# A state space mixer that projects its time steps before the convolved tiles, and takes the output norm of four groups at once inside the next projection

## The chip, the cores and the metric

The kernel runs on one core of a Trainium2 chip. The metric is the device time of one execution in microseconds (us), the median of three runs. The engines are TensorE (PE, with PEld for its weight loads), VectorE (DVE), ScalarE (ACT), GpSimd (POOL) and SyncE (SP), which issues most of the DMAs.

## The reference, cut to what matters

Two transformer-like blocks are computed in one launch. The change lies in the mixer of the first block: 512 tokens (lat) and 256 context tokens (ctx), width 1024. All of it is in 32-bit floats.

```python
p_l = modulate(rmsnorm(h_lat, norm1[i]), sh1_l, sc1_l) @ w_in[i]
p_c = modulate(rmsnorm(h_ctx, norm1[i]), sh1_c, sc1_c) @ w_in[i]
# ssd_inputs, for both: gate z, convolved xbc, two sets of 16 step sizes
z = proj[..., :OFF_XBC]
xbc = jax.nn.silu(dwconv_centred(proj[..., OFF_XBC:OFF_DT], conv_w, conv_b))   # 5 taps
dt_f = jax.nn.softplus(dt_raw[..., :SSD_HEADS] + dt_bias[0])
dt_b = jax.nn.softplus(dt_raw[..., SSD_HEADS:] + dt_bias[1])
# ssd_scan in chunks of 128, forwards and backwards, from dt, a = dt * a_head, xs, B, C; then
o_ssd_l = group_rmsnorm((y + xs * d_skip) * jax.nn.silu(z), norm_g, SSD_GROUPS)  # 4 groups of 256
# hyena: another 3072 columns of the projection, 3-tap convolution, two long convolutions
o_hy_l = hyena(p_l[..., OFF_HY:], ...)
mix_l = jnp.concatenate([o_ssd_l, o_hy_l], axis=-1) @ w_out[i]
```

## The kernel before, in words

Activations lie with their features on the 128 partitions and the tokens along the row. A projection (`project`, L262 on) makes one tile of 128 output features: eight slices of 128 inputs, three matmuls in reduced fp32 for each (`trio`, L253 to L255), because the weights and the input are split into a high and a low part. The weight tile comes by DMA into `raw_ring` (six slots of 128x1024, filled by SP strictly in one order, `load_order`), ACT casts the high part (`Weights.hi`, L235), POOL subtracts for the low part (`Weights.lo`, L243), and the two stand in one of three `pair` buffers. `tile_order` gives each tile a lead: how many tiles ahead its split stands in the program. Each engine runs its own list in order and waits on counters of the others; `everyone(k, eng, stage)` makes an engine wait until all four have ended a stage.

The stages that matter here:

- **inproj** (functions `..._inproj`). PE projects eight tiles of the gate z, then sixteen tiles that are convolved (`win` 8 to 23), the first twelve for lat and ctx (512 + 256 columns), the last four for lat alone. For each of the sixteen, ACT copies the tile from PSUM to `raw` (L520), DVE runs the five taps (L431, L434), ACT applies Silu (L525 to L532), PE transposes the result (`turned`, L280), DVE copies it out (L418, L419, L422). ACT copies a tile only after the Silu of the tile before it. DVE also computes the modulation, 32 `step`s (L407), each reading one slot of the ring: eight between the end of the input's split and the convolved tiles, sixteen with the convolved tiles, eight (40 to 47) after them. Last comes `wdt`, the 32 columns of step sizes: projected by PE after `win` 23, bias on DVE (L448), transposed, and turned into softplus by a chain of DVE instructions of 192 columns (L452 to L478) with one Exp on ACT (L536). The next stage needs its result `a` at once.
- **ssd1, ssd2**: the scan. At its end `zT` holds the gated output (L703).
- **ssd**: the group norm of `zT`. ACT squares eight tiles (L785), PE multiplies them by a matrix of 1/256 so that every partition of a 128x512 bank holds the mean (L259, in full fp32), DVE adds epsilon (L797), ACT takes the root (L789), DVE takes four reciprocals (L802) and multiplies (L711). `scalar_norms`, `vector_norms` and `tensor_norms` are used again by the hyena part.
- **hyena**, first part: 24 more projected tiles, `win` 24 to 47, each copied by ACT (L1051) and convolved by DVE with three taps (L952, L954, L956). On two of them DVE also computes `angles` (L936 to L946). All four engines enter it through `everyone(..., "ssd")`. POOL first issues three DMAs for the transform matrices (`dft`, L1084). The weights of `win` 24 to 26 are split only behind that wait.

## Time and profile before

| | |
|---|---|
| median of 3 runs | 5046.19 us (5045.71 to 5047.88) |
| the profiled execution | 5075.65 us, of which its span is 5073.8 us |
| PE busy | 4531.9 us, 89% of the span |
| DVE busy | 2722.1 us, 54% |
| POOL busy | 1754.2 us, 35% |
| ACT busy | 1515.6 us, 30% |
| mean granted clock of PE, of 1 | 0.94 |

The stages of the mixer in that execution, in us from the start of the span: the gate's tiles to about 125, the convolved tiles to 278, the steps and what is left of inproj to 298, the scan to 459, the norm to 495, the 24 tiles of the hyena projection to 632. The times of single instructions below come from this one profiled execution, which is 0.6% longer than the median run.

### The profile page before, as it was taken

What the parts mean: (1) busy time and instruction counts of PE and PEld (TensorE: products, weight loads), DVE (VectorE), ACT (ScalarE), POOL (GpSimd) and SP (SyncE); (2) the same over time, 40 slices, a digit from 0 to 9 for tenths busy, and PEclk for the clock granted to TensorE, in tenths of its full rate; (3) what the DMA queues carried; (4) which work ended last, traced back from release to release, by engine and by line L of the source; (5) the groups of instructions that cost most, each with busy time, mean ns of one, the idle gap of its engine ahead of it and who ended that gap; (6) DMA issues with size and microseconds to landing.
All of it is one profiled execution on the core that took longest, in us unless ns stands there. A gap on an engine that the chain in (4) does not pass through costs nothing.

```text
span 5073.8 us, 51551 instructions
## 1 busy us (share of the span) xinstructions
PE 4531.9 (89%) x20654; PEld 3503.6 (69%) x20654; DVE 2722.1 (54%) x4692; ACT 1515.6 (30%) x2546; POOL 1754.2 (35%) x933
## 2 busy tenths in 40 slices
PE   7866988787669999999999979997999979986998
PEld 3755845356557888888888856666888857754886
DVE  3875745349887666654443334563443450485334
ACT  3211211034752222222222233443212122343222
POOL 2243432025964444444444421003223225102442
PEclk9987999898789999999999999988999989998999
DMA  5210200121235544444433210001122202101331
GB/s 203 96 67 31 92 29 17 62 72 46 117 155 197 171 161 166 164 155 166 171 136 121 100 37 16 13 1 50 55 63 63 63 29 63 34 1 54 92 96 49
DMA packets 170618, 440.76 MB, mean 87 GB/s; under 512 B 12203, under 2 KB 78955, under 8 KB 167436
## 3 DMA queue, kind: packets, MB, share of 16 engines
q1 hardware_dynamic: 168060, 422.61, 24.5%
q0 software_dynamic: 2320, 14.86, 0.8%
q8 instruction: 164, 2.69, 0.2%
q14 instruction: 74, 0.61, 0.0%
HBM read 401.77 MB, written 35.65 MB: 86 GB/s over the span
## 4 chain that ended last, share of the span: by engine, by line
PE 60%; DVE 7%; ACT 2%; issue 1%; DMA 0%; POOL 0%; DVEq 0%; ACTq 0%; POOLq 0%
PE psum L253 17%; PE psum L255 17%; PE psum L254 17%; PE psum L259 7%; DVE st L2112 2%; PE psum L280 1%; DVE Pd L2138 1%; DVE k L802 1%; DVE X L1785 0%; ACT P L2183 0%; DVE ffl L1725 0%; DVE Pe L2136 0%; DVE rstd L1765 0%; DVE X L1788 0%; DVE st L2119 0%
## 5 line engine op out<-in xcount | busy, mean ns | idle before, releaser
L243 POOL TENSOR_TENSOR pair<-raw_ring,pair 128x1024 fp32r<-128x1024 f32 (+1 forms) x503 | 1243.8, 2488 | 2297.2 <-ACT pair L235 2297.1
L235 ACT CAST pair<-raw_ring 128x1024 fp32r<-128x1024 f32 (+1 forms) x503 | 510.3, 1044 | 370.7 <-PE psum L255 321.7
L253 PE MATMUL psum<-pfh,pair 128*128 128x512 f32 x1152 | 460.0, 399 | 27.4 <-POOL pair L243 25.8
L1578 DVE SCALAR_TENSOR_TENSOR h<-psum,mods,h 128x512 f32<-128x512 f32 x512 | 373.0, 748 | 184.4 <-PE psum L255 182.9
L255 PE MATMUL psum<-pfh,pair 128*128 128x512 f32 x1152 | 458.8, 398 | 0.0
L254 PE MATMUL psum<-pfl,pair 128*128 128x512 f32 x1152 | 458.4, 398 | 0.0
L253 PE MATMUL psum<-ffh,pair 128*128 128x512 f32 (+1 forms) x1056 | 382.3, 362 | 45.3 <-DVE ffl L1725 45.3
L253 PE MATMUL psum<-Ah,pair 128*128 128x512 f32 x1024 | 408.6, 399 | 9.8 <-DVE h L1578 4.8
L255 PE MATMUL psum<-Ah,pair 128*128 128x512 f32 x1024 | 407.9, 398 | 0.0
L254 PE MATMUL psum<-Al,pair 128*128 128x512 f32 x1024 | 407.8, 398 | 0.0
L254 PE MATMUL psum<-ffl,pair 128*128 128x512 f32 (+1 forms) x1056 | 380.3, 360 | 0.0
L255 PE MATMUL psum<-ffh,pair 128*128 128x512 f32 (+1 forms) x1056 | 379.8, 360 | 0.0
L1636 ACT ACTIVATE gl<-psum 128x512 f32<-128x512 f32 x122 | 73.1, 599 | 832.6 <-PE psum L255 832.6
L1571 DVE TENSOR_TENSOR pr<-gl,Gb 128x512 f32<-128x512 f32 x128 | 91.4, 714 | 342.2 <-ACT gl L1636 324.3
L253 PEld LDWEIGHTS psum<-pfh,pair 128*128 128x128 f32 x1152 | 218.7, 190 | 79.3 <-issue 23.1
L259 PE MATMUL psum<-o,o 128*128 128x128 f32 x1024 | 177.1, 339 | 101.6 <-POOL o L1503 77.2
L253 PEld LDWEIGHTS psum<-ffh,pair 128*128 128x128 f32 x1056 | 200.6, 190 | 84.1 <-issue 39.1
L254 PEld LDWEIGHTS psum<-pfl,pair 128*128 128x128 f32 x1152 | 218.8, 190 | 50.5
L255 PEld LDWEIGHTS psum<-pfh,pair 128*128 128x128 f32 x1152 | 218.6, 190 | 50.5
L259 PEld LDWEIGHTS psum<-o,o 128*128 128x128 f32 x1024 | 161.4, 243 | 117.6 <-POOL o L1503 78.5
L1948 DVE SCALAR_TENSOR_TENSOR X<-psum,mods,X 128x512 f32<-128x512 f32 (+1 forms) x264 | 170.8, 661 | 121.0 <-PE psum L255 121.0
L253 PEld LDWEIGHTS psum<-Ah,pair 128*128 128x128 f32 x1024 | 194.4, 190 | 56.3 <-issue 9.6
(517 smaller groups left out, 9305.0 us busy)
## 6 DMA issues: line engine op xcount, KB each, us to landing
raw_ring<-wmod SPq DMA_DIRECT2D x144, 512.0 KB, 5.2
raw_ring<-peeru SPq DMA_DIRECT2D x128, 512.0 KB, 4.2
raw_ring<-peerv SPq DMA_DIRECT2D x128, 512.0 KB, 4.8
gates<-stage SPq DMA_DIRECT2D x16, 2048.0 KB, 6.4
Gb<-gates SPq DMA_DIRECT2D x32, 1024.0 KB, 9.2
raw_ring<-win SPq DMA_DIRECT2D x48, 512.0 KB, 4.4
raw_ring<-wgate SPq DMA_DIRECT2D x44, 512.0 KB, 3.5
raw_ring<-wup SPq DMA_DIRECT2D x44, 512.0 KB, 3.6
```

The source lines that it names most:

```text
L235: ac.e.copy(self.pair(t)[0], k.R.of(t)).then_inc(*k.A.up("hi", t))
L243: po.e.tensor_tensor(lo, k.R.of(t), hi.bitcast(F), ALU.subtract).then_inc(*k.G.up("lo", t))
L253: e.matmul(out, w[0], x[0], start=first, stop=False, skip_group_check=True)
L254: e.matmul(out, w[0], x[1], start=False, stop=False, skip_group_check=True)
L255: return e.matmul(out, w[1], x[0], start=False, stop=last, skip_group_check=True)
L259: return e.matmul(out, w, x, start=first, stop=last, skip_group_check=True)
L280: return e.transpose(out, src, k.sq["ident"][0:n, 0:n])
L1571: e.tensor_tensor(v3(y, 32), v3(x, 32), G4[:, :, n % 4, :], ALU.mult).then_inc(*V.up("act", n))
L1578: e.scalar_tensor_tensor(out=h[:, j, :], in0=B.of(("down", gi, j)), scalar=m[:, 40 + j, 0:1], in1=h[:, j, :], op0=ALU.mult, op1=ALU.add).t ...
L1636: e.activation(gelus(k, n), B.of((("U", n), 0)), AF.Gelu).then_inc(*A.up("gelu", n))
L1948: e.scalar_tensor_tensor(out=x, in0=B.of((key, "down", gi, q, s))[:, 0:b - a], scalar=m[:, 40 + q, s:s + 1], in1=x, op0=ALU.mult, op1=ALU. ...
L2112: e.tensor_reduce(s[:, 0:1], bank[:, 0:u.n], AX, ALU.max).then_inc(*V.up())
```

## The change

It does three things.

- `wdt` gets buffers of its own. It is loaded by SP behind `wmod` 47, ACT casts it after the eighth gate tile, POOL subtracts before the low part of the tile that `win` 8 asks for, and PE projects it ahead of `win` 8. Its transposes follow `win` 8. The short DVE part stands behind convolved tile 1, the long part behind tile 3, and ACT's Exp ahead of the copies of tile 3. The buffers of the chain move to `Btok`, which is written only from tile 8 on. Modulation steps 40 to 47 stand beside steps 16 to 23. With `wdt` out of `tile_order`, `win` 24 takes its place: it is split during inproj.
- The stage `ssd` is gone. The squares are taken by ACT after hyena tiles 0 and 1, in eight buffers of their own. `tensor_means` puts the means of the four groups on four partitions of one bank (behind tile 2), DVE adds epsilon (behind tile 3), ACT takes one root (behind tile 4), DVE one reciprocal of 4x512 (behind tile 5), `tensor_back` spreads each group's row over 128 partitions with four matmuls (behind tile 7), and DVE multiplies two tiles of `zT` behind each of tiles 8 to 11.
- PE enters hyena without a wait, the others wait for `ssd2`. The `dft` DMAs are issued by POOL behind tile 10, since the squares use that memory.

The core of the diff (the body of the step-size chain is the same in both, and only moved):

```diff
 def tensor_inproj(k, pe):
...
+    pe.wait_ge(k.G.at("lo", "wdt"))
+    for s, (a, b) in enumerate(SEG2):
+        bank = B.take(("wdt", s))
+        pe.wait_ge(B.free(("wdt", s)))
+        for q in range(8):
+            i = trio(e, bank[0:32, 0:b - a], [w[:, 32 * q:32 * q + 32] for w in k.wdt], k.fx(q, s), q == 0, q == 7)
+        i.then_inc(*P.up("wdt", s))
     for j in range(16):
         project(k, pe, ("win", 8 + j), k.fx, SEG2 if j < 12 else SEG1)
+        if j == 0:
+            bank = B.take("dtT")
+            pe.wait_ge(V.at("dtin", 1), B.free("dtT"))
...
-    project(k, pe, ("wdt",), k.fx, SEG2, M=32)
...
 def vector_inproj(k, dv):
...
     for j in range(8):
         step(16 + j)
+        step(40 + j)
...
+    dt_in()
     for j in range(16):
...
+        if j == 1:
+            dt_one()
+        if j == 3:
+            dt_two()
         step(24 + j)
-    for j in range(40, 48):
-        step(j)
...
 def scalar_inproj(k, ac):
...
     for j in range(16):
         raw, acc, si = k.raws[j % 2], k.accs[j % 2], k.sil[j % 2]
+        if j == 0:
+            ac.wait_ge(k.R.at("wdt"))
+            e.copy(k.wdt[0], k.R.of("wdt")).then_inc(*A.up("hi", "wdt"))
         W.hi(ac, ("win", 8 + j))
+        if j == 3:
+            x, ex, s, q, p, dt, a, AA = k.dtp
+            ac.wait_ge(V.at("dtabs"))
+            e.activation(ex, ex, AF.Exp, scale=-1.0).then_inc(*A.up("dtexp"))
+            e.activation(AA[:, 0:32], k.row["alog"], AF.Exp).then_inc(*A.up("alog"))
...
 def pool_inproj(k, po):
...
     for j in range(1, 24):
+        if j == 8:
+            po.wait_ge(k.A.at("hi", "wdt"))
+            e.tensor_tensor(k.wdt[1], k.R.of("wdt"), k.wdt[0].bitcast(F), ALU.subtract).then_inc(*G.up("lo", "wdt"))
+            k.R.over("wdt", G.now())
         W.lo(po, ("win", j))
-    W.lo(po, ("wdt",))
...
+def tensor_means(k, pe, key, n, sq, place, rows, among=(0, 1, 2, 3, 4, 5, 6, 7)):
+    bank = k.B.take((key, "ms"), 1, among)
+    pe.wait_ge(k.B.free((key, "ms")))
+    for i in range(n):
+        pe.wait_ge(k.A.at(key, "sq", i))
+        mm(pe.e, bank[0:rows, :], place(i), sq(i), i == 0, i == n - 1).then_inc(*k.P.up(key, "sq", i))
...
 def tensor_hyena(k, pe):
     e, P, V, A, G, B, R = pe.e, k.P, k.V, k.A, k.G, k.B, k.R
-    everyone(k, pe, "ssd")
     for j in range(24):
         project(k, pe, ("win", 24 + j), k.fx, SEG1)
+        if j == 2:
+            tensor_means(k, pe, "ssdn", 8, lambda i: k.zsq[i], lambda i: k.vec["z256"][:, 3 - i // 2:7 - i // 2], 4)
+        if j == 7:
+            for g in range(4):
+                tensor_back(k, pe, "ssdn", g, k.sq["ident"][0:4, g:g + 1].to_broadcast([4, 128]), k.zr[0:4, :])
...
 def vector_hyena(k, dv):
...
+        if j == 3:
+            vector_means(k, dv, "ssdn", 8, 4, k.zr)
+        if j == 5:
+            vector_inverse(k, dv, "ssdn", 4, k.zr)
+        if 8 <= j < 12:
+            g = j - 8
+            dv.wait_ge(P.at("ssdn", "back", g))
+            for z in (2 * g, 2 * g + 1):
+                e.scalar_tensor_tensor(out=k.z3[:, z, :], in0=k.z3[:, z, :], scalar=k.vec["ssd_norm"][:, z:z + 1], in1=B.of(("ssdn", "back", g)),
+                                       op0=ALU.mult, op1=ALU.mult).then_inc(*V.up())
+            B.over(("ssdn", "back", g), V.now())
...
 def pool_hyena(k, po):
...
-    everyone(k, po, "ssd")
-    for dst, src, t in zip((k.dft1, k.dft2, k.dft3), ("dft1", "dft2", "dft3"), k.dft):
-        e.dma_start(dst, k.d[src]).then_inc(*t.up())
+    everyone(k, po, "ssd2")
...
+        if j == 10:
+            po.wait_ge(P.at("ssdn", "back", 3))
+            for dst, src, t in zip((k.dft1, k.dft2, k.dft3), ("dft1", "dft2", "dft3"), k.dft):
+                e.dma_start(dst, k.d[src]).then_inc(*t.up())
```

What this makes of the order of instructions, at three places. In the names, `pair` is a split weight tile, `y` the scan's output, `fh` and `fl` the split input. PE at the end of the scan, before:

```order
L280 MATMUL psum<-squares_1920_49,y_1024_132 128x128 x3
L280 MATMUL psum<-squares_1920_49,y_1024_132 128x128 [waits scalar_done]
L280 MATMUL psum<-squares_1920_49,y_1024_132 128x128 x3
L259 MATMUL psum<-xl_4096_83,squares_1920_49 128x512 [waits scalar_done,vector_done,tensor_done]
L259 MATMUL psum<-xl_4096_83,squares_1920_49 128x512 [waits scalar_done] x7
L253 MATMUL psum<-fh_512_67,pair_2048_59 128x512 [waits scalar_done,pool_done,vector_done,tensor_done]
L254 MATMUL psum<-fl_512_75,pair_2048_59 128x512
```

and after:

```order
L281 MATMUL psum<-squares_1920_49,y_1024_134 128x128 x3
L281 MATMUL psum<-squares_1920_49,y_1024_134 128x128 [waits scalar_done]
L281 MATMUL psum<-squares_1920_49,y_1024_134 128x128 x3
L254 MATMUL psum<-fh_512_67,pair_2048_58 128x512
L255 MATMUL psum<-fl_512_75,pair_2048_58 128x512
L256 MATMUL psum<-fh_512_67,pair_2048_58 128x512
```

The norm's matmuls between the transposes and the first projected tile are gone, and that tile has no wait of its own left. ACT at the same place, before (`M` is the scan's decay, `xl` here the squares, `BT` the mean):

```order
L732 ACTIVATE M_512_130<-psum 128x512 [waits tensor_done]
L785 ACTIVATE xl_4096_83<-zT_4096_66 128x512 [waits scalar_done,pool_done,vector_done,tensor_done]
L785 ACTIVATE xl_4096_83<-zT_4096_66 128x512 x7
L789 ACT_TABLE_LOAD
L789 ACTIVATE BT_2048_84<-BT_2048_84 128x512 [waits vector_done] x4
L235 CAST pair_2048_59<-raw_ring_6144_57 128x1024 [waits scalar_done,ring_loaded1,vector_done,tensor_done]
L235 CAST pair_2048_60<-raw_ring_6144_57 128x1024 [waits ring_loaded2]
```

and after:

```order
L747 ACTIVATE M_512_132<-psum 128x512 [waits tensor_done]
L236 CAST pair_2048_59<-raw_ring_6144_57 128x1024 [waits pool_done,scalar_done,ring_loaded2,vector_done,tensor_done]
L236 CAST pair_2048_60<-raw_ring_6144_57 128x1024 [waits ring_loaded3]
L1111 COPY hraw_516_153<-psum 128x512 [waits pool_done,tensor_done]
L1115 ACTIVATE zsq_512_142<-zT_4096_66 128x512
L1115 ACTIVATE zsq_512_143<-zT_4096_66 128x512
```

The casts stand ahead of the squares, and there are two, since `win` 24 was split before. DVE behind convolved tile 3 (`acc` is the convolution's sum, `crow` belongs to a modulation step), before:

```order
L418 COPY xl_4096_83<-psum 128x4x128 [waits tensor_done]
L419 COPY xc_2048_88<-psum 128x2x128
L407 ISA raw_ring_6144_57,mods_96_52<-raw_ring_6144_57,crow_23696_1024_118 128x1024 [waits ring_loaded5]
L407 ISA mods_96_52 128x1
L431 TENSOR_SCALAR acc_768_110<-raw_776_108,vecs_657_50 128x512 [waits scalar_done]
```

and after, up to the last but one instruction of the chain:

```order
L430 COPY xl_4096_83<-psum 128x4x128 [waits tensor_done]
L431 COPY xc_2048_88<-psum 128x2x128
L455 TENSOR_SCALAR Btok_3072_89<-Btok_3072_89 128x192
L457 RECIPROCAL Btok_3072_89<-Btok_3072_89 128x192 [waits vector_done]
L459 TENSOR_TENSOR Btok_3072_89<-Btok_3072_89 128x192 [waits vector_done]
L461 TENSOR_TENSOR Btok_3072_89<-Btok_3072_89 128x192 [waits vector_done]
L463 TENSOR_SCALAR Btok_3072_89<-Btok_3072_89 128x192 [waits vector_done]
L466 SCALAR_TENSOR_TENSOR Btok_3072_89<-Btok_3072_89 128x192 [waits vector_done] x7
L468 SCALAR_TENSOR_TENSOR Btok_3072_89<-Btok_3072_89 128x192 [waits vector_done]
L469 TENSOR_SCALAR Btok_3072_89<-Btok_3072_89 128x192
L471 SCALAR_TENSOR_TENSOR small_1600_86<-Btok_3072_89 128x192 [waits vector_done]
L474 TENSOR_SCALAR Btok_3072_89<-Btok_3072_89 128x32
```

The step-size chain stands between the copies of one tile and the modulation step that goes ahead of the next.

## Rows read from the trace of the kernel before

**Rows 1.** Stretch 495.5 to 640: length, busy us of each engine, clock, DMA.

```profile
495.50:640.00 144.50, 144.48 (x604) 114.01 (x604) 100.89 (x91) 37.94 (x50) 61.08 (x25) 0.98 0.27 98
```

**Rows 2.** PE in time order: start, us, instruction, count, idle before and its releaser.

```profile
456.95 1.09 PE L280 MATMUL psum<-squares,y 128*128 128x128 f32 x8 [1.31 <-DVE y L698]
460.06 10.10 PE L259 MATMUL psum<-xl,squares 128*128 128x512 f32 x16 [2.02 <-ACT xl L785]
495.52 0.77 PE L253 MATMUL psum<-fh,pair 128*128 128x512 f32 x1 [25.36 <-POOL pair L243]
...
500.30 0.39 PE L255 MATMUL psum<-fh,pair 128*128 128x512 f32 x1
...
635.01 1.02 PE L259 MATMUL psum<-raw_ring,h 128*128 128x512 f32 x2
635.87 1.02 PE L259 MATMUL psum<-raw_ring,h2n 128*128 128x512 f32 x2
```

**Rows 3.** DVE and POOL in the norm and behind it.

```profile
470.80 3.34 DVE L802 RECIPROCAL BT<-BT 128x512 f32<-128x512 f32 x1
...
488.32 1.42 DVE L711 SCALAR_TENSOR_TENSOR zT<-zT,vecs,BT 128x512 f32<-128x512 f32 x2
490.41 1.66 POOL L1084 DMA_DIRECT2D dft<-dft  x3 [41.28 <-DVE zT L711]
...
493.02 6.99 POOL L243 TENSOR_TENSOR pair<-raw_ring,pair 128x1024 fp32r<-128x1024 f32 x3
```

**Rows 4.** DVE during the hyena projection.

```profile
521.95 2.78 DVE L956 SCALAR_TENSOR_TENSOR hv<-hraw,vecs,hacc 128x512 f32<-128x512 f32 x1
526.08 0.55 DVE L952 TENSOR_SCALAR hacc<-hraw,vecs 128x512 f32<-128x512 f32 x1 [1.35 <-ACT hraw L1051]
...
527.45 2.78 DVE L956 SCALAR_TENSOR_TENSOR hv<-hraw,vecs,hacc 128x512 f32<-128x512 f32 x1
...
561.14 4.21 DVE L944 SCALAR_TENSOR_TENSOR h<-hr,h 64x512 f32<-64x512 f32 x3
```

**Rows 5.** DVE and PE from the last convolved tile to the scan.

```profile
277.67 1.22 DVE L407 CUSTOM_DVE_ANT_0 raw_ring<-raw_ring,crow 128x1024 f32<-128x1024 f32 x1
...
291.45 0.26 DVE L457 TENSOR_SCALAR small<-small 128x192 f32<-128x192 f32 x1 [0.43 <-ACT small L536]
...
298.01 0.36 DVE L478 TENSOR_TENSOR small<-small 128x192 f32<-128x192 f32 x1
...
298.47 2.85 PE L259 MATMUL psum<-small,squares 128*128 128x96 f32 x12 [8.24 <-DVE small L478]
```

**Rows 6.** PE, first and last matmul of `wdt` (48 in all).

```profile
271.99 0.39 PE L253 MATMUL psum<-fh,pair 128*32 128x512 f32 x1
...
280.19 0.28 PE L255 MATMUL psum<-ch,pair 128*32 128x256 f32 x1
```

**Rows 7.** DVE, POOL and ACT: a convolved tile, a weight split, a table load.

```profile
163.07 2.01 DVE L431 TENSOR_SCALAR acc<-raw,vecs 128x512 f32<-128x512 f32 x1 [0.54 <-ACT raw L520]
...
162.35 2.44 POOL L243 TENSOR_TENSOR pair<-raw_ring,pair 128x1024 fp32r<-128x1024 f32 x1 [7.74 <-ACT pair L235]
...
463.57 1.28 ACT L789 ACT_TABLE_LOAD   x1
```

**Rows 8.** DVE and POOL at convolved tile 14, where `wdt` is split.

```profile
269.16 0.58 DVE L431 TENSOR_SCALAR acc<-raw,vecs 128x512 f32<-128x512 f32 x1 [0.34 <-ACT raw L520]
...
268.71 0.74 POOL L243 TENSOR_TENSOR pair<-raw_ring,pair 128x256 fp32r<-128x256 f32 x1 [4.47 <-ACT pair L235]
```

**Rows 9.** DVE and ACT during the gate's tiles, up to the first convolved tile.

```profile
95.16 3.43 DVE L407 CUSTOM_DVE_ANT_0 raw_ring<-raw_ring,crow 128x1024 f32<-128x1024 f32 x1
...
107.55 1.22 DVE L407 CUSTOM_DVE_ANT_0 raw_ring<-raw_ring,crow 128x1024 f32<-128x1024 f32 x1 [2.25 <-DMA raw_ring<-wmod]
...
134.07 0.55 DVE L431 TENSOR_SCALAR acc<-raw,vecs 128x512 f32<-128x512 f32 x1 [19.42 <-ACT raw L520]
...
125.34 0.60 ACT L513 ACTIVATE zT<-psum 128x512 f32<-128x512 f32 x1 [3.96 <-PE psum L255]
```

More of the change, by code:

```diff
@@ L316, in lay_inproj @@
     k.mrow = m.take("mrow", 2048)
+    k.wdt = [m.rounded("wdt", 256) for _ in range(2)]
     m.at = at_small
@@ L322, in lay_inproj @@
     sm = k.small
-    k.dtp = [sm[:, 192 * i:192 * i + 192] for i in range(8)]
-    k.dt, k.a = v3(k.dtp[5], 32), v3(k.dtp[6], 32)
+    k.dtT = Btok[0:32, 0:768]
+    k.dtp = [Btok[:, 768 + 192 * i:960 + 192 * i] for i in range(8)]
+    k.dt1, k.a1 = sm[:, 1024:1216], sm[:, 1216:1408]
+    k.dt, k.a = v3(k.dt1, 32), v3(k.a1, 32)
     k.inputs1 = ((0, 512, k.f3, k.gain_l, k.fh, k.fl), (512, 768, k.c3, k.gain_c, k.ch, k.cl))
@@ L532, in scalar_inproj @@
             e.activation(si[:, 512:768], acc[:, 512:768], AF.Silu).then_inc(*A.up("silu1", j))
-    W.hi(ac, ("wdt",))
-    x, ex, s, q, p, dt, a, AA = k.dtp
-    ac.wait_ge(V.at("dtabs"))
-    e.activation(ex, ex, AF.Exp, scale=-1.0).then_inc(*A.up("dtexp"))
-    e.activation(AA[:, 0:32], k.row["alog"], AF.Exp).then_inc(*A.up("alog"))
     A.name("end", "inproj")
@@ L705, in vector_ssd @@
     V.name("end", "ssd2")
-    everyone(k, dv, "ssd2")
-    def finish(g, r):
-        for i in (2 * g, 2 * g + 1):
-            z = k.z3[:, i, :]
-            e.scalar_tensor_tensor(out=z, in0=z, scalar=k.vec["ssd_norm"][:, i:i + 1], in1=r, op0=ALU.mult, op1=ALU.mult).then_inc(*V.up())
-    vector_norms(k, dv, "ssdn", 4, k.BTflat, finish)
-    V.name("end", "ssd")
 def scalar_ssd(k, ac):
@@ L765, in pool_ssd, with vector_means, scalar_means, vector_inverse @@
     G.name("end", "ssd2")
-    everyone(k, po, "ssd2")
-    G.name("end", "ssd")
+def tensor_means(k, pe, key, n, sq, place, rows, among=(0, 1, 2, 3, 4, 5, 6, 7)):
[4 more added lines that the diff above has]
+        mm(pe.e, bank[0:rows, :], place(i), sq(i), i == 0, i == n - 1).then_inc(*k.P.up(key, "sq", i))
+def vector_means(k, dv, key, n, rows, out):
+    dv.wait_ge(k.P.at(key, "sq", n - 1))
+    dv.e.tensor_scalar(out[0:rows, :], k.B.of((key, "ms"))[0:rows, :], EPS, None, ALU.add).then_inc(*k.V.up(key, "ms"))
+    k.B.over((key, "ms"), k.V.now())
+def scalar_means(k, ac, key, rows, out):
+    ac.wait_ge(k.V.at(key, "ms"))
+    ac.e.activation(out[0:rows, :], out[0:rows, :], AF.Sqrt).then_inc(*k.A.up(key, "sqrt"))
+def vector_inverse(k, dv, key, rows, out):
+    dv.wait_ge(k.A.at(key, "sqrt"))
+    dv.e.reciprocal(out[0:rows, :], out[0:rows, :]).then_inc(*k.V.up(key, "inverse"))
+def tensor_back(k, pe, key, g, w, out, among=(0, 1, 2, 3, 4, 5, 6, 7)):
+    bank = k.B.take((key, "back", g), 1, among)
+    pe.wait_ge(k.V.at(key, "inverse"), k.B.free((key, "back", g)))
+    mm(pe.e, bank, w, out).then_inc(*k.P.up(key, "back", g))
 def tensor_norms(k, pe, key, groups, tiles, sq, mean):
@@ L813, in lay_hyena @@
     k.dft1, k.dft2, k.dft3 = m.take("dft1", 2304), m.take("dft2", 2048), m.take("dft3", 2048)
+    at = m.at
+    m.at = k.base + 24576
+    k.zsq, k.zr = [m.take("zsq", 512) for _ in range(8)], m.take("zr", 512)
+    m.at = at
     k.KC, k.KS, k.NY = v3(k.dft1[:, 0:1024], 512), v3(k.dft1[:, 1024:2048], 512), v3(k.dft1[:, 2048:2304], 128)
@@ L1052, in scalar_hyena @@
         B.over((("win", 24 + j), 0), A.now())
+        if j < 2:
+            for z in range(4 * j, 4 * j + 4):
+                e.square(k.zsq[z], k.z3[:, z, :]).then_inc(*A.up("ssdn", "sq", z))
+        if j == 4:
+            scalar_means(k, ac, "ssdn", 4, k.zr)
         if j == 11:
@@ L2836, in tile_order @@
 def tile_order(d):
-    t = [(("win", j), d["win"][j], 1024, 2 if j < 23 else 1, 3, 0) for j in range(24)] + [(("wdt",), d["wdt"], 256, 0, 3, 0)]
+    t = [(("win", j), d["win"][j], 1024, 2 if j < 23 else 1, 3, 0) for j in range(24)]
     t += [(("win", j), d["win"][j], 1024, min(2, 47 - j), 3 if j < 45 else 1, 0) for j in range(24, 48)]
@@ L2887, in load_order @@
         raw(("wmod", 16 + j), d["wmod"][j])
-    for j in range(24, 32):
-        raw(("wmod", 16 + j), d["wmod"][j])
-    use(("wdt",))
+        if j < 8:
+            raw(("wmod", 40 + j), d["wmod"][24 + j])
+        if j == 7:
+            raw("wdt", d["wdt"], 256)
     for j in range(24):
```

98 lines of the change are left out of this document (50 added, 48 removed).

## The prediction

> **What bounds the kernel now.** I read the stages in order of time and asked in each what PE waits for, since PE is busy for 89% of the span and the rest of the program is untouched by this change. In the hyena projection PE is busy for 144.48 of 144.5 us [rows 1]: there PE is the bound, and each of its microseconds counts. Right before it lies the largest hole of the mixer: the last transposes of the scan start at 456.95 and end at 458.04, and the first projected tile starts at 495.52, behind POOL's weight split [rows 2]. In these 37.5 us PE runs 10.1 us of matmuls for the norm; the rest is DVE's reciprocals and multiplies (3.34 and 1.42 us for each of four groups) and then POOL's DMA issues and splits [rows 3]. The second hole is at the end of inproj: the last convolution is done at 277.67, and the scan's first matmul starts at 298.47, behind the last instruction of the step-size chain [rows 5]. Between lie nine modulation steps and that chain, all on DVE. The convolved tiles themselves are not bound by PE: they go round a loop of DVE's five taps, ACT's Silu, cast and copy, and back to DVE, in which DVE waits only 0.54 us per tile [rows 7]. So work put on DVE there is nearly free for 0.54 us per tile and costs its full time beyond that.
>
> **The output norm, part by part.** *Removed:* the 37.5 us between 458.04 and 495.52 [rows 2]. PE goes straight into `win` 24, whose split was done in inproj. Nothing else can hold it there: the tile has no wait. The next two tiles need two casts and two splits, which ACT and POOL begin when DVE ends the scan, within about 1 us; three splits took 6.99 us [rows 3], so the second of two is there some 7 us after 458, and PE needs it only after two tiles of 5.5 us (the period in rows 4, 527.45 less 521.95).
>
> *Added on PE:* eight matmuls for the means and four to spread the roots, 128x512 in full fp32. One is two records and takes 0.86 us start to start (635.87 less 635.01) [rows 2], so 12 x 0.86 = 10.3 us, all of it on the path, since PE is the bound. The upper end is the norm's own eight, 10.10 us [rows 2], part of it at the lower clock: 1.26 each, 15.1 us.
>
> *The clock:* before, the projection began after 25 us of idle PE, and its matmuls became short only at 500.30 (0.77 us at first, 0.39 then) [rows 2]. After, PE comes out of the scan, which is full of small waits, so I expect the same few slow microseconds once, and take no gain or loss; bounds 2 us either way.
>
> *Added on ACT, DVE, POOL:* ACT gets eight squares on an engine that is busy for 38 of 144.5 us [rows 1]. DVE waits 1.35 us per tile [rows 4], 32 us over 24 tiles. It gets one reciprocal (3.34), four pairs of multiplies (1.42 each) [rows 3] and one addition: about 10 us. That fits in sum but not in place: behind tiles 8 to 11 each iteration takes 1.42 us and has 1.35, and `angles` falls behind tile 9, whose three steps alone took 4.21 us [rows 4]. There DVE comes about 5 us later than now. PE sees it through PSUM: the four spread banks are freed only by the multiplies, and tiles 13 and 14 of the 24 take the last two of these banks. I put 1.5 us on that, bounds 0 and 4. The three `dft` DMAs cost POOL 1.66 us [rows 3] behind tile 10, where it has over 2 us of idle per tile (5.5 less a split, 2.44 [rows 7]), and their data is first read after the projection, over 60 us later: nothing. If that cover were gone, it would be the transfer itself, which today runs beside the hole's splits.
>
> Sum of this part: -37.5 + 10.3 + 1.5 = **-25.7 us**, bounds -18 and -29.
>
> **The step sizes, part by part.** *Projected first:* `wdt` took PE from 271.99 to 280.47, 8.5 us, hidden at the end under DVE's steps [rows 6]. Now it stands before `win` 8, and DVE waits for `win` 8 with nothing to do (it sat idle for 19.42 us until 134.07 [rows 9]), so the whole loop of the convolved tiles starts 8.5 us later: **+8.5**. Ahead of it PE waits for the split of `wdt`: ACT's Silu of the last gate tile (0.60 us) [rows 9], a cast, at most as long, and POOL's 0.74 us [rows 8], in a row from the end of `win` 7: **+1.9**, bounds 1.3 and 4 (POOL can be held up by a step).
>
> *The chain in the loop:* the short part is two instructions of 0.36 us [rows 5], against 0.54 us of slack: +0.3. The long part ran from 291.45 to 298.37, 6.9 us [rows 5]. Less the slack that is 6.4, and it also comes to lie under POOL's split of 2.44 us, which DVE ran into with one instruction before (2.01 us for what takes 0.58 alone) [rows 7, 8]: **+7.0**, bounds 5 and 7.5. The Exp needs a table load of 1.28 us [rows 7] ahead of the copies of tile 3; but while ACT loads it, POOL's split ends, and DVE's first instruction, which was stretched by it by 1.4 us, is not any more: **+0.4**, bounds 0 and 2. The load back to Silu lies in ACT's wait for DVE.
>
> *The split of `win` 24 in place of `wdt`:* at tile 14 DVE's first instruction took 0.58 us beside POOL's short split, against 2.01 beside a long one [rows 7, 8]. With ACT's cast, four times as wide, 0.65 us longer by my estimate: **+2.1**, bounds 0 and 2.5.
>
> *The tail:* before, 298.47 less 277.67 = 20.8 us; after, one step of 1.22 us [rows 5], one addition and the wait, 1.5 us: **-19.3**, bounds 1 us either way. Of this 9.2 us are the eight steps 40 to 47. They go to where DVE idles for 19.42 us [rows 9]; there they need eight more ring slots in the time of eight gate tiles, three loads per 5.5 us in place of two. A step takes 1.22 us free and 3.43 when it meets POOL's split [rows 9]; one of each makes 4.65 us per tile, which is under 5.5, so the ring keeps up: nothing.
>
> Sum of this part: 8.5 + 1.9 + 0.3 + 7.0 + 0.4 + 2.1 - 19.3 = **+0.9 us**, bounds -4 and +6. Moving the steps and the chain pays for itself and no more: what is gained at the end is given back at the start of the loop.
>
> On the terms of 7.0 and 2.1: in rows 7 and 8 a DVE instruction beside a weight split takes 2.01 us in place of 0.58, and ends when the split does. The Trainium skill (SBUF — State Buffer, section "🔬 SBUF: two separate sides") says that DVE in its two-port modes or with two SBUF inputs and GpSimd lock a shared port pair for a whole instruction and the loser blocks fully; the trace agrees. By that rule the chain's term would be 7.4, and with no blocking at all 5.0; the sum would be 0.4 higher or 2 lower. On the Exp: the table load in rows 7 is 1.28 us. The Trainium skill (ScalarE: Activation LUTs, section "What ACT_TABLE_LOAD costs") gives 1283 ns and a drain of about 1380 ns besides; no drain shows in this case's trace, and by the page's figure the term would be about 1.4 us more.
>
> **The forecast.** -25.7 + 0.9 = -24.8 us. The profiled execution took 5075.65 us (span 5073.8) and would take 5050.9; it is 0.6% longer than the median run, which scales the difference by 0.994 to 24.6: 5046.2 - 24.6 = **5021.6 us**.
>
> **The rivals.** *1. The loop gives nothing back.* If DVE's chain fell into waits that rows 7 do not show, and the loop made up the late start because PE is further ahead, the tail's 19.3 us would be kept but for the 8.5: 25.7 + 10.8 = 36 us, 5010. Against it: each tile needs DVE's time anyway, and no lead of PE shortens that. Chance 0.07.
>
> *2. The projection loses PE as its bound.* With lags of DVE around tiles 5 to 14, ACT's in-order list (copies wait for DVE's convolution two tiles back, casts stand behind them) could delay the splits, so that PE waits 3 us on each of some four tiles: +12 us, 5034. For it: the 1.35 us of slack is small against 3.34 and 4.21 in one place [rows 3, 4]. Against it: before, `angles` made the same kind of lag, and PE was still busy for all of 144.5 us [rows 1]. Chance 0.08.
>
> *3. The ring starves the gate's tiles, and the kernel is slower.* SP loads in one order, so a late step holds back the weight tiles behind it. If every step met a split (3.43) and also waited 2.25 us for its load, as one did [rows 9], two steps would take 11.4 us per tile against 5.5: 5.9 x 8 = 47 us, and 5068 in all. It decides from 4.3 us per step on (25 us lost over eight tiles); between 2.75 and 4.3 it only eats into the gain. Against it: the steps that waited were early, not late, for DVE had nothing else to do. Chance 0.04.
>
> *4. The early start does not come about.* Were `win` 24 split only after the scan, PE would still wait for the cast and the split, some 4 us, then for the next: 5027. The order of instructions shows no wait there. Chance 0.02, inside the range.
>
> **How the numbers follow.** The forecast has 0.79. Its own bounds, -29 - 4 and -18 + 6, are ends that would all have to fall on one side; with most of them I get 5014 to 5034. That also holds rivals 2 and 4, and leaves out rivals 1 and 3 (0.11) and the outer bounds, some 0.06. A measurement of this kernel can tell about 0.2%, 10 us, from no change. Faster by more than that are the forecast, rivals 1 and 4 and most of 2: 0.94. Rival 3 is split: 0.03 slower, the rest, with the worst of 2, within 0.2%: 0.03.
>
> **What would show it.** Right: PE's first `win` 24 matmul follows the last transpose within 1 us; the 24 tiles with the norm take some 12 us more than before; the first tap starts some 10 us later than 134; the iteration with the long chain is some 7 us longer than the others; from the last tap to the scan 1.5 us. Wrong: idle of PE behind POOL's splits in the gate's tiles or between hyena tiles 3 and 14; a tail that still waits for anything but one step.

## The result, and the profile after

The changed kernel takes 4992.58 us (median of 4 runs, 4987.86 to 4997.6) against 5047.03 us of the kernel before (5045.71 to 5048.19): a ratio of 0.9888, 95% interval 0.9875 to 0.9902. That is 54.5 us less, where the forecast had 24.6 less and a range that ended at 5014. The profiled execution took 4987.86 us (span 4986.1).

In the mixer nearly all came as forecast. PE goes from the scan's last transposes straight into the projection, the 24 tiles keep PE busy, and the tail of inproj is gone. The views are PE's work in order of time, and the projection's stretch (its columns as in [rows 1]); they answer to [rows 2], [rows 1], [rows 5], [rows 6] and [rows 9]:

```profile
454.11 1.09 PE L281 MATMUL psum<-squares,y 128*128 128x128 f32 x8 [1.31 <-DVE y L722]
454.96 0.48 PE L254 MATMUL psum<-fh,pair 128*128 128x512 f32 x1
...
454.96:604.90 149.94, 149.53 (x620) 113.92 (x619) 101.21 (x99) 45.97 (x62) 60.96 (x28) 0.99 0.27 100
```

```profile
125.97 0.40 PE L254 MATMUL psum<-fh,wdt 128*32 128x512 f32 x1 [2.41 <-DVE mods L418]
...
134.11 0.28 PE L256 MATMUL psum<-ch,wdt 128*32 128x256 f32 x1
...
297.93 2.85 PE L260 MATMUL psum<-small,squares 128*128 128x96 f32 x12 [8.43 <-DVE mods L499]
```

The last transposes are followed by the first projected tile, `wdt` is projected ahead of the convolved tiles, and the scan's first matmul waits only for DVE's last step and one addition (L499).

The rest did not come from the two parts. The costliest groups of PE's instructions (line, operation, tiles, shape, count | busy us, mean ns of one | idle before) are the split matmuls of the expert stage, whose code the change does not touch. The kernel before, then after:

```profile
L255 PE MATMUL psum<-pfh,pair 128*128 128x512 f32 x1152 | 458.8, 398 | 0.0
L255 PE MATMUL psum<-Ah,pair 128*128 128x512 f32 x1024 | 407.9, 398 | 0.0
```

```profile
L256 PE MATMUL psum<-pfh,pair 128*128 128x512 f32 x1152 | 449.4, 390 | 0.0
L256 PE MATMUL psum<-Ah,pair 128*128 128x512 f32 x1024 | 400.0, 391 | 0.0
```

Part of this step from 398 to 390 ns belongs to the execution of the kernel before that was profiled, 5075.65 us long: in another, near the median, both groups take 395 ns (run again, below). `pfh`, `pfl` and `Ah`, `Al` are the high and low parts of the two inputs that PE streams past the weights in that stage.

A stretch in the middle of that stage says it more sharply: in 500 us in which PE is never idle and has its full clock, it does 2145 matmuls before and 2208 after, one every 0.233 and every 0.226 us. Before, then after (columns as in [rows 1]; the first number in brackets counts PE's matmuls):

```profile
2000.00:2500.00 500.00, 500.00 (x2145) 405.00 (x2144) 284.07 (x397) 139.56 (x179) 225.01 (x88) 1.00 0.48 162
```

```profile
2000.00:2500.00 500.00, 500.00 (x2208) 414.01 (x2207) 283.15 (x399) 143.58 (x184) 234.99 (x92) 1.00 0.50 169
```

What the change did to that stage is one thing that the list of its three parts and the prediction both pass over: it adds 52 columns (`z64`, `z256`, `z128`) to the table of small vectors. Only the seven of `z256` are used. All buffers behind the table lie 48 floats (192 bytes) higher, while the ring of raw tiles and the split weights (`pair`), which are laid out from the top of the memory, stay where they are.

### The profile page after: what moved, and what is told of

Its sections match the earlier page's. It is cut to its first block, busy times and chain, and to the rows that moved or that the text cites. A ratio compares the mean times of both kernels' runs of the same rounds, so it can differ in the third digit from the quotient of the medians.

```text
span 4986.1 us, 51556 instructions
## 1 busy us (share of the span) xinstructions
PE 4467.1 (90%) x20662; PEld 3482.5 (70%) x20662; DVE 2713.5 (54%) x4686; ACT 1516.3 (30%) x2545; POOL 1753.2 (35%) x933
## 4 chain that ended last, share of the span: by engine, by line
PE 60%; DVE 8%; ACT 2%; issue 1%; DMA 0%; POOL 0%; DVEq 0%; ACTq 0%; POOLq 0%
PE psum L254 17%; PE psum L256 17%; PE psum L255 17%; PE psum L260 7%; DVE st L2179 2%; PE psum L281 1%; DVE Pd L2205 1%; DVE k L843 1%; DVE X L1852 0%; ACT P L2250 0%; DVE ffl L1792 0%; DVE Pe L2203 0%; DVE rstd L1832 0%; DVE X L1855 0%; DVE st L2186 0%
## 5 line engine op out<-in xcount | busy, mean ns | idle before, releaser
L244 POOL TENSOR_TENSOR pair<-raw_ring,pair 128x1024 fp32r<-128x1024 f32 x502 | 1241.7, 2487 | 2272.0 <-ACT pair L236 2271.8
L236 ACT CAST pair<-raw_ring 128x1024 fp32r<-128x1024 f32 x502 | 510.1, 1046 | 369.3 <-PE psum L256 314.4
L254 PE MATMUL psum<-pfh,pair 128*128 128x512 f32 x1152 | 451.5, 392 | 27.8 <-POOL pair L244 26.5
L256 PE MATMUL psum<-pfh,pair 128*128 128x512 f32 x1152 | 449.4, 390 | 0.0
L254 PE MATMUL psum<-Ah,pair 128*128 128x512 f32 x1024 | 400.6, 391 | 10.7 <-DVE Al L1640 5.2
L256 PE MATMUL psum<-Ah,pair 128*128 128x512 f32 x1024 | 400.0, 391 | 0.0
```

What stands on the lines that cost most here:

```text
L236: ac.e.copy(self.pair(t)[0], k.R.of(t)).then_inc(*k.A.up("hi", t))
L244: po.e.tensor_tensor(lo, k.R.of(t), hi.bitcast(F), ALU.subtract).then_inc(*k.G.up("lo", t))
L254: e.matmul(out, w[0], x[0], start=first, stop=False, skip_group_check=True)
L256: return e.matmul(out, w[1], x[0], start=False, stop=last, skip_group_check=True)
```

## The experiments

All times are medians; each ratio is against runs of the kernel before on the same chip.

| run | what it is | us | ratio (95% interval) |
|---|---|---|---|
| layout | before, 52 columns more | 5014.20 | 0.9942 (0.9925 to 0.9958) |
| both664 | after, without 45 unused columns | 5025.19 | 0.9954 (0.9938 to 0.9971) |
| norm | norm part alone | 5025.45 | 0.9952 (0.9935 to 0.9968) |
| steps | steps part alone | 5047.23 | 1.0006 (0.9992 to 1.0021) |
| up8 | working buffers +32 bytes | 5082.04 | 1.0069 (1.0052 to 1.0085) |
| up16 | +64 bytes | 5058.23 | 1.0021 (1.0012 to 1.0031) |
| up32 | +128 bytes | 5054.42 | 1.0010 (1.0001 to 1.0020) |
| up112 | +448 bytes | 5008.95 | 0.9920 (0.9903 to 0.9936) |
| down48 | ring and weights -192 bytes | 5020.47 | 0.9949 (0.9932 to 0.9966) |
| pairs48 | weights alone -192 bytes | 5013.52 | 0.9938 (0.9922 to 0.9955) |
| ahup16 | layout, second expert buffers +64 bytes | 5024.35 | 0.9951 (0.9934 to 0.9967) |
| glup16 | the same without `Ah`, `Al` | 5013.97 | 0.9937 (0.9917 to 0.9957) |
| bothlow | both664, weights -192 bytes | 4994.07 | 0.9888 (0.9872 to 0.9905) |
| again | before, unchanged | 5048.94 | 1.0006 (0.9993 to 1.0019) |
| spread | after, chain cut up | 4993.57 | 0.9891 (0.9874 to 0.9907) |
| late | spread, `wdt` inside the tiles | 4986.46 | 0.9877 (0.9861 to 0.9894) |
| aligned | after, last stages moved | 4988.35 | 0.9882 (0.9866 to 0.9899) |
| best | late and aligned | 4977.06 | 0.9857 (0.9840 to 0.9873) |

**Which part it is.** The theory was that the place of the buffers gives what the mixer does not show; the rivals were that it comes with a part, or that executions differ. layout adds the table entries and nothing that uses them; both664 takes the two unused ones out again, so that the rounding to eight floats puts all buffers back where they were:

```diff
 layout:   +        ("z64", 30), ("z256", 7), ("z128", 15)]
 both664:  -        ("z64", 30), ("z256", 7), ("z128", 15)]
           +        ("z256", 7)]
```

> The kernel before with only the 52 unused columns added to the table of small vectors, so that every buffer behind it lies 48 floats higher; no instruction is changed. Theory A (the part of the gain that the changed stages do not show, some 24 us, comes from where the buffers lie): 5017 to 5025 us, and the 128x512 matmuls of the later stages as short as after (391 ns in place of 398). Theory B (it comes with the norm or the steps themselves) and theory C (it is a difference between executions or chips): both 5047 within 5, matmuls at 398.

> The changed kernel with the two unused tables of 45 columns taken out again, so that the buffers lie where they lay before; norm and steps as in the change. Theory A: the gain falls to what the mixer shows, 5015 to 5022 us. Theories B and C: as the changed kernel, 4988 to 4998.

> The norm part alone (win 24 split at the end of inproj behind wdt), buffers where they lay before. The prediction's sum: -25.7, 5021 us. From the mixer's anchors in the trace of after (hole gone, projection 10.3 longer, first matmuls at once at full clock): -27 to -29, 5018 to 5020. If the unexplained 24 us come with this part: about 4995.

> The steps part alone, buffers where they lay before. The prediction's sum: +0.9, 5048 us. From the anchors (end of inproj 0.6 earlier, scan 3 to 4 shorter): 5043 to 5046. If the unexplained 24 us come with this part: about 5020.

layout gained 33.6 us without one changed instruction; both664, with all changed instructions, gained 22.6. norm alone gave 22.3 and steps alone nothing. So the theory holds, and 22.3 + 0.5 + 33.6 = 56.4 us is what the whole change gave (54.5), within the errors. The single times missed what was expected by a few microseconds (layout 3 under its range, both664 3 above its, norm 4 above), but each interval is some 8 us wide to either side. layout's stretch shows the same count of matmuls as after:

```profile
2000.00:2500.00 500.00, 500.00 (x2208) 414.15 (x2207) 287.82 (x404) 143.56 (x184) 235.58 (x93) 1.00 0.51 169
```

**Alignment or distance.** Before, the working buffers began 64 bytes past a multiple of 128 and, what is another thing, 64 bytes (modulo 256) past the place of the split weights. up8, up16, up32 and up112 put floats ahead of the working buffers; down48 and pairs48 leave these and lower the weights:

```diff
 upN:      -    m.at += -m.at % 8
           +    m.at += -m.at % 8 + N
                k.base = m.at
 pairs48:  -        m.at = 53184 - 6 * 1024 - 2048 * (s + 1)
           +        m.at = 53136 - 6 * 1024 - 2048 * (s + 1)
```

> The kernel before with the working buffers 16 floats (64 bytes) higher; the ring of raw tiles, the split weights and the tables stay. Theory A1 (the matmuls run faster when the buffers begin at a multiple of 128 bytes; before they begin 64 bytes off one, in layout at one): as layout, 5014 us. Theory A2 (what counts is the distance between the working buffers and the split weights, which was a multiple of 1024 bytes in layout): as before, 5047. Theory A3 (any shift frees it by some other match): 5014.

> The same with 32 floats (128 bytes). A1: as before, 5047, for the buffers are 64 bytes off again. A2: 5047. A3: 5014.

> The kernel before with the ring and the split weights 48 floats (192 bytes) lower and the working buffers where they were: the distance is that of layout, the working buffers stay 64 bytes off a multiple of 128, and now the weights are too. A1: 5047 (or more, if the weights count as well). A2: 5014.

> The working buffers 8 floats (32 bytes) higher, 96 bytes past a multiple of 128 and no longer at a multiple of 64. A1: not faster than before; 5047, or slower if a multiple of 64 already helps. A2: 5047.

up16, which begins at a multiple of 128 bytes, was not faster but 10 us slower, and down48, whose working buffers did not move at all, was nearly as fast as layout: it is the distance (A2), not the alignment. A2 in its plain form missed too, since it had put up8, up16 and up32 at 5047: the distances other than 0 differ among themselves. up8, the only one whose distance is no multiple of 64, is the slowest of all.

> The kernel before with only the split weights 48 floats (192 bytes) lower; working buffers and ring stay. If the distance between moving data and split weights is what counts: as layout and down48, 5014 to 5020 us, 2208 matmuls between 2000 and 2500 us. If it is the distance to the ring of raw tiles (written by the loads, read by ACT and POOL): as before, 5047, and 2145 to 2186 matmuls.

> The kernel before with the working buffers 112 floats (448 bytes) higher: the distance to the split weights is a multiple of 256 bytes, but not of 512. If a multiple of 256 is enough: 5014. If it has to be one of 512 or 1024, as in layout: not faster than before, 5045 to 5060.

pairs48 settles that the ring has no part in it. up112 has a distance of 256 bytes modulo 512 and is as fast as layout. So a multiple of 256 bytes is enough. For the distance modulo 256 of the expert stage, the matmuls in the stretch and the time of the whole kernel (in which the last stages have distances of their own, see aligned): 0, 2208, 5009 to 5020; 64 (before), 2145 or 2186 (see again), 5047; 96, 2145, 5082; 128, 2153, 5058; 192, 2144, 5054. The stretches of pairs48 and up16:

```profile
2000.00:2500.00 500.00, 500.00 (x2207) 414.01 (x2207) 287.41 (x404) 143.41 (x184) 235.64 (x93) 1.00 0.51 169
```

```profile
2000.00:2500.00 500.00, 500.00 (x2153) 405.35 (x2152) 285.96 (x399) 139.51 (x179) 226.31 (x89) 1.00 0.48 162
```

**Whose data it is.** All working buffers had moved together, so it could have been PE's moving data or the buffers that DVE, ACT and the loads use. From layout, where the distance is 0, two kernels take a part back to 64: ahup16 `Ah` and `Al` with all that lies behind them, glup16 only what lies behind them (`gl`, `pr` and others, which DVE, ACT, POOL and the loads use, and PE does not):

```diff
 ahup16:   -    m.at = low
           +    m.at = low + 16
                k.Ah, k.Al = [...], [...]
 glup16:   +    m.at += 16
                k.gl, k.pr = [...], [...]
```

> The kernel layout with only the expert stage's second group of buffers (Ah and Al, and behind them gl, pr, Gb, crow, junk) 16 floats (64 bytes) higher; pfh and pfl stay. If what counts is where a matmul's own moving data lies against its weights: the matmuls on Ah and Al go from 391 to 395 to 399 ns, those on pfh and pfl stay at 391, and the time rises by half of what layout gained, to 5022 to 5030 us. If it is the other engines' buffers that collide with PE: both groups become slower.

> As ahup16, but Ah and Al stay too: only gl, pr, Gb, crow and junk, which DVE, ACT, POOL and the loads use, lie 16 floats higher. If the moving data counts: as layout, 5014 us, all four groups at 391 ns. If the other engines' buffers count: 5022 to 5045.

glup16 cost nothing and ahup16 cost 10 us. Four runs of each overlap in time (5005.6 to 5023.7 and 5021.0 to 5026.1), but the traces do not: the expert stage takes 1354.9 us in layout and in glup16 and 1365.3 in ahup16, and the stretch has 2208, 2208 and 2190 matmuls. So it is the moving data. The stretch of ahup16:

```profile
2000.00:2500.00 500.00, 500.00 (x2190) 410.94 (x2189) 286.28 (x402) 141.83 (x182) 234.49 (x92) 1.00 0.51 168
```

The groups of layout, then those of ahup16:

```profile
L254 PE MATMUL psum<-Ah,pair 128*128 128x512 f32 x1024 | 400.3, 391 | 10.0 <-DVE h L1579 4.9 <-DVE Al L1574 4.0 <-POOL pair L244 1.1
L255 PE MATMUL psum<-Al,pair 128*128 128x512 f32 x1024 | 399.8, 390 | 0.0
L256 PE MATMUL psum<-Ah,pair 128*128 128x512 f32 x1024 | 399.6, 390 | 0.0
```

```profile
L254 PE MATMUL psum<-Ah,pair 128*128 128x512 f32 x1024 | 405.4, 396 | 9.8 <-DVE h L1579 4.8 <-DVE Al L1574 4.0 <-POOL pair L244 1.0
L256 PE MATMUL psum<-Ah,pair 128*128 128x512 f32 x1024 | 402.9, 393 | 0.0
...
L255 PE MATMUL psum<-Al,pair 128*128 128x512 f32 x1024 | 399.6, 390 | 0.0
...
L256 PE MATMUL psum<-pfh,pair 128*128 128x512 f32 x1152 | 451.0, 392 | 0.0
```

The matmuls on `Ah` go from 391 and 390 to 396 and 393 ns; those on `Al`, moved as far, and on `pfh`, not moved, hardly change. Which of the three matmuls of a trio is slow is not fixed by the distance: in again, with all of them 64 bytes off, it is the first one that stays at 390. No run explains the pattern. The same groups in again:

```profile
L255 PE MATMUL psum<-Ah,pair 128*128 128x512 f32 x1024 | 404.6, 395 | 0.0
L254 PE MATMUL psum<-Al,pair 128*128 128x512 f32 x1024 | 402.7, 393 | 0.0
L253 PE MATMUL psum<-Ah,pair 128*128 128x512 f32 x1024 | 399.2, 390 | 9.9 <-DVE h L1578 4.8 <-DVE Al L1573 4.0 <-POOL pair L243 1.1
```

The Trainium skill (SBUF — State Buffer, section "🔬 SBUF: two separate sides") says that PE never waits on anyone for its SBUF port; glup16 agrees, as far as the place of the others' buffers goes, and leaves PE's own two readings, weights and moving data. That these two collide is the nearest reading of pairs48 and ahup16, and is argued, not shown: no record shows one read waiting for another.

**Does it add up.**

```diff
 bothlow = both664 with the edit of pairs48
 again   = the kernel before
```

> both664 (norm and steps, tables as before) with only the split weights 48 floats lower, as in pairs48. If the parts simply add: 5025 less the 30 to 34 us of pairs48 and layout, 4991 to 4995 us, the time of the changed kernel without its unused columns. If the columns did something else besides: some other time.

> The kernel before, unchanged, profiled again. The execution that was profiled took 5075.65 us, 29 more than the median. If the matmul spacing differs from one execution to the next: an execution of 5045 to 5055 us shows some 2186 matmuls between 2000 and 2500 us (as norm did) in place of 2145, and the expert stage takes about 1367 us in place of 1393. If that stage is the same in all executions, 2145 again.

bothlow is as fast as the changed kernel, without its 45 unused columns: for the time they did nothing but move the buffers. again explains why the first pair of traces, 5075.65 and 4987.86 us, differs by 88 us where the medians differ by 54. Its profiled execution took 5049.26 us, the expert stage in it 1367.7 us in place of 1393.4, which is nearly all of the 26 us between the two executions, and the stretch has 2186 matmuls:

```profile
2000.00:2500.00 500.00, 500.00 (x2186) 410.24 (x2185) 288.34 (x402) 141.49 (x181) 235.12 (x92) 1.00 0.50 170
```

At a distance of 64 bytes the pace of the matmuls differs from one execution to the next (2145, 2186); at 0 it was 2207 or 2208 in the profiled executions of all eleven kernels that had it.

**The loop of the convolved tiles, and a better version.** spread cuts the long chain, 17 instructions, into ones and twos behind tiles 4 to 15. late puts them behind tiles 8 to 15, and also puts `wdt` in two pieces behind `win` 9 and `win` 12, and the transposes one tile later. In both, the chain gets other buffers:

```diff
 spread:   -        if j == 3:
           -            dt_two()
           +        if j >= 4:
           +            dt_some((2, 1, 1, 2, 1, 1, 2, 1, 1, 2, 1, 2)[j - 4])
 ...
 late:     +        if j == 1:
           +            wdt(0)
           +        if j == 4:
           +            wdt(1)
 ...
           -        if 0 < j < 13:
           -            turned(j - 1)
           +        if 1 < j < 14:
           +            turned(j - 2)
```

> The changed kernel with the long step-size chain cut up: one or two of its 17 instructions behind each of tiles 4 to 15 in place of all behind tile 3. By the term of 7.0 us for the chain: the iteration of tile 4 loses its 6 to 7 us, the others get 0.1 to 0.4 each where two instructions exceed the 0.54 us of slack: 4 to 5 us faster than the changed kernel, 4988 (by its median of 4992.6). If DVE's time in sum is what counts and there is no slack to use: no change.

> As spread, and wdt no longer ahead of win 8 but in two pieces behind win 9 and win 12, the transposes of a tile two tiles behind its projection in place of one, the chain behind tiles 8 to 15. By the terms of 8.5 and 1.9 us, less 1.7 us that DVE waits at the third tile: first tap 10.4 us earlier than after (133 in place of 143), the stage 8 to 9 us shorter, in all 11 to 13 us faster than the changed kernel: 4980. If the loop is short of PE's time and not of DVE's, the two pieces come back as DVE's waits for ACT's copies: 4988 or more.

spread missed: it gained nothing that the runs can tell. The first taps of tiles 0 and 15 are 146.96 us apart in place of 149.59, so 2.6 of the expected 4 to 5 us came in the loop, less than the 10 us by which the runs of after differ. In the loop, with one or two instructions more per tile, DVE's first tap takes 2.1 to 2.6 us in most tiles where it took 2.0; that it has moved further under POOL's split is read from the order, not tested.

late brought the first tap to 132.56 us from 143.17, and the stretch from inproj's first matmul to the last of the stages ahead of the scan is 8.7 us shorter (251.6 for 260.3), as expected. The whole missed its 11 to 13 us: 6 arrived in the median. In the two profiled executions nothing arrived (4988.17 and 4987.86): the scan took 125.3 us for 120.1, at a granted clock of 0.82 where after had 0.87, and the stretch from the first `hh` to the first `ofh` matmul, which late does not touch, 532.5 for 526.6. After, then late:

```profile
335.10:455.20 120.10, 94.73 (x641) 89.87 (x642) 73.92 (x71) 19.12 (x32) 59.85 (x40) 0.87 0.00 1
```

```profile
326.60:451.90 125.30, 99.83 (x641) 95.03 (x642) 73.40 (x71) 19.11 (x32) 59.20 (x40) 0.82 0.00 1
```

aligned and best use the finding on the distance. Small tiles of 80 floats put the moving data of the last stages 64 bytes further than that of the first, so the change left these at 64:

```diff
 aligned, best:  +    m.at += 48
                      k.rstd = m.take("rstd", 768)
                      k.top = m.at
```

> The changed kernel with 48 more unused floats ahead of the buffers of the last stages (from 2860 us on). There small tiles put the moving data 64 bytes off the weights' place; the 48 floats take it to a multiple of 256 bytes. In up32, which had it there, the stage from the first ofh matmul on took 843.8 us against 850.4 in layout, and the one on ofh as weights 0.227 us start to start against 0.233. If the rule holds: 7 to 15 us faster than the changed kernel, 4978 to 4986. If 64 bytes off does no harm: 4992.

> The kernel late with the same 48 floats: both gains, 7 to 15 us under late, 4972 to 4980 us. If the rule does not hold in the last stages: 4986.

The last long stage (first `ofh` matmul to last `ffh` one) took 844.0 us in aligned for 850.9, and up32, where it is at 0 as well, took 843.8. But the median of the whole moved by 4.2 us only, less than the 7 to 15 expected and within the spread of the runs. The traces show why: the same 48 floats move the stage ahead of it too, and from the first `hh` to the first `ofh` matmul, a feed-forward of 768 columns, aligned took 533.4 us for 526.6, so that 6.8 of the 6.9 us went again. In that stage the rule does not hold as it does in the others: at a distance of 0 it took 533.4 us in all three kernels that had it (aligned, best, up32), at 64 from 524.9 to 534.2 in ten kernels, at 128 from 538.5 to 541.0 in five executions. No run says why. best took 4977.06 us, 15.5 under the changed kernel, and is the fastest of all.

## Why the prediction was right and wrong

Stage lengths in us, worked out from the starts of the matmuls named (the scan and the projection to the end of their last matmul; the expert stage from the first `Ah` matmul to the last), in the profiled executions. again stands for before, since its execution is near the median:

| stage | again | after | norm | layout |
|---|---|---|---|---|
| first matmul of inproj to the first on `aL` or `CT`, near 334 | 258.1 | 260.3 | 259.1 | 257.8 |
| from there to the end of the scan | 123.7 | 120.1 | 125.3 | 123.2 |
| hole behind it | 37.5 | -0.2 | 0.3 | 37.4 |
| hyena projection | 136.7 | 147.0 | 148.1 | 135.5 |
| expert stage | 1367.7 | 1354.8 | 1367.7 | 1354.9 |
| first `hh` to first `ofh` matmul | 538.5 | 526.6 | 541.0 | 524.9 |
| from there to the last `ffh` | 858.2 | 850.9 | 856.4 | 850.4 |

**The hole** was to go whole, -37.5: it did, by 37.7. **The twelve full-fp32 matmuls and the PSUM wait** were to cost 10.3 + 1.5 = 11.8, **the clock** nothing, with bounds of 2 us. At the same place of the buffers the projection became 11.4 longer (norm less again) or 11.5 (after less layout). The sum is right; under it are two movements of the clock that the prediction did not have, and that they nearly cancel is luck. In the trace of after the twelve matmuls take 10.6 us start to start, and tiles 12 to 14 take 1.0 more than in layout, 0.4 of it idle time of PE. At the start 2.2 us are gained: the first twelve matmuls take 2.8 us for 5.0. Then 1.75 us are lost: the tile behind the spread matmuls, which have four rows of data, takes 7.28 us for 5.53 in layout, and some of its matmuls 0.63 us for 0.39. The views are the start of the projection before, with a granted clock of 0.51, and the spread matmuls and the stretch behind them after, with one of 0.72:

```profile
495.52:500.30 4.78, 4.78 (x12) 3.82 (x13) 0.00 (x0) 0.00 (x0) 4.49 (x2) 0.51 1.00 419
```

```profile
505.89 3.70 PE L260 MATMUL psum<-zr,squares 4*128 4x512 f32 x8
...
511.12 0.63 PE L254 MATMUL psum<-fh,pair 128*128 128x512 f32 x1
```

```profile
510.00:516.00 6.00, 6.00 (x21) 4.75 (x20) 1.26 (x2) 0.00 (x0) 0.00 (x0) 0.72 0.00 0
```

**Rivals 2, 3 and 4** did not occur: PE is idle for 0.4 us in the whole projection, follows the last transpose without a gap, and waits 0.8 us in all among the gate's tiles up to the `wdt` matmuls.

**`wdt` first**, +8.5 and +1.9: it takes 8.4 us (125.97 to 134.4), behind a wait of 2.41, which is above the 1.9 and inside its bounds: POOL's split of `wdt` ends just before, and took 1.31 us beside one of DVE's steps, for the 0.74 of the sum. The first tap stands at 143.17 for 134.07, and as inproj began 1.5 us earlier the loop starts 10.6 later, for 10.4 by the sum. POOL's split:

```profile
124.57 1.31 POOL L576 TENSOR_TENSOR wdt<-raw_ring,wdt 128x256 fp32r<-128x256 f32 x1 [0.36 <-ACT wdt L540]
```

**The chains, Exp and the long split** were 7.0 + 0.3 + 0.4 + 2.1 = 9.8, and from the first tap to that of the last tile it is 149.59 us for 139.99: +9.6. The sum is right, its parts less so. DVE around tiles 3 and 4, answering to [rows 7] and [rows 5]:

```profile
174.63 0.55 DVE L485 TENSOR_SCALAR acc<-raw,vecs 128x512 f32<-128x512 f32 x1 [2.32 <-ACT raw L549]
...
183.25 1.99 DVE L459 TENSOR_TENSOR Btok<-Btok 128x192 f32<-128x192 f32 x1
...
189.76 0.36 DVE L476 TENSOR_TENSOR small<-small,Btok 128x192 f32<-128x192 f32 x1
...
191.18 0.54 DVE L485 TENSOR_SCALAR acc<-raw,vecs 128x512 f32<-128x512 f32 x1
```

The period of tile 2 is 12.58 us, +2.4 over the 10.17 of the others, for the 0.4 of the Exp: the table load delays the copy (2.32 us of idle for 0.54), and the tap's own stretch before it is not saved in that period. That of tile 3 is 16.55, +6.4: the chain takes 8.5 us, one instruction stretched to 1.99 under the split (it ends at 185.24, 0.2 behind the split), less the idle and less the stretch that the tap does not have (0.55 for 2.01). Tile 4 then has 8.71, -1.5. Together +7.3 for 7.7. ACT's table load shows 1.28 us and its next instruction follows at once:

```profile
171.02 1.03 ACT L236 CAST pair<-raw_ring 128x1024 fp32r<-128x1024 f32 x1
172.07 1.28 ACT L545 ACT_TABLE_LOAD   x1
173.36 0.37 ACT L545 ACTIVATE Btok<-Btok 128x192 f32<-128x192 f32 x1
```

So the drain that the Trainium skill (ScalarE: Activation LUTs, section "What ACT_TABLE_LOAD costs") puts beside the load is not to be seen here either. The last three periods, with the long split, are 2.3 longer, for 2.1.

**The tail**, -19.3: from the last step's start to the scan's first matmul it is 1.56 us (296.37 to 297.93) for 20.8, so -19.2. The terms of the steps part add up to 10.6 + 9.6 - 19.2 = +1.0 us for +0.9; the table's +2.2 has 1.3 more from behind the scan's first matmul, which no run explains. Rival 1 is out with the loop's 9.6, and the steps part alone changed the time by -0.5 us.

**What failed is a term put at nothing in the first paragraph of the prediction**, where it takes "the rest of the program" as "untouched by this change". By the parts that it names the change gives 22.6 us (both664), 5025.2 us: 3.6 above the forecast of 5021.6 and well inside its range. The missing term is the 48 floats: -33.6 us by layout. In the traces of again and after it is -12.9 in the expert stage, where the moving data went from 64 bytes off to 0, and the two last rows of the table, -11.9 and -7.3, where it went from 128 to 64 bytes off; layout has these too. Of the three, the -11.9 is the least sure, since that stage took anything from 524.9 to 534.2 us at 64 bytes off. **The scan**, -3.6, is no term of either part and not of the layout: its instructions are the same, aligned and spread had the same order and took 122.9, and over all the traces its length goes with the clock granted in it (0.87 for 120.1 us, 0.85 for 122.8 and 122.9, 0.83 for 123.1 to 124.0, 0.82 for 124.5 to 125.3). That the profiled execution of after had the shortest one is luck. These are aligned and norm:

```profile
337.50:460.40 122.90, 97.41 (x641) 92.44 (x642) 73.53 (x71) 19.11 (x32) 59.41 (x40) 0.85 0.00 1
```

```profile
335.10:460.30 125.20, 99.73 (x640) 94.77 (x640) 73.39 (x71) 19.11 (x32) 59.21 (x40) 0.82 0.00 1
```

## What to carry to other kernels

In a kernel that PE bounds, read a diff for what it does to addresses, even where it only lengthens a table: 192 bytes were worth more here than both intended parts together. Try the moving data of long runs of 128x512 matmuls and their weights at the same place modulo 256 bytes, and measure each stage by itself: here it gave 13 us in the expert stage and 7 in the last one, and nothing in the feed-forward between them. When comparing two versions, hold the layout fixed, or give each the layout that it likes. In a loop whose engine has 0.5 us of slack per turn, moving work into it gives back what it saves elsewhere; here the gain of the steps part was nothing, and the stage became shorter only with `wdt` out of the way of the first tile as well (late).
